# Prompt delta rule: the inverse turned instead of multiplied twice, and both lanes in the same step

## Chip, cores and metric

The kernel runs on one core of a Trainium2 chip. The metric is the time of one execution in device microseconds (us), lower is better. A core has five engines with a queue of instructions each: TensorE (PE, its weight loads are shown as PEld), VectorE (DVE), ScalarE (ACT), GpSimd (POOL) and SyncE (SP, which issues transfers). An engine takes its instructions in the order of the program and waits on semaphores.

## The reference, cut to what matters

The whole program is one inference step of a two-layer decoder. The change lies in layer 0, in the gated delta rule for the prompt: 512 tokens, 6 heads of 128, from a state of zeros.

```python
gamma = jnp.exp(jnp.where(incl, G[..., :, None] - G[..., None, :], -jnp.inf))
kk = jnp.einsum('nbhik,nbhjk->nbhij', kc, kc)
a_mat = jnp.where(strict, kk * gamma * bc[..., :, None], 0.0) + jnp.eye(chunk, dtype=F32)
rhs = jnp.concatenate([vc * bc[..., None], kc * (bc * jnp.exp(G))[..., None]], axis=-1)
sol = lax.linalg.triangular_solve(a_mat, rhs, left_side=True, lower=True, unit_diagonal=True)
u, w = sol[..., :DV], sol[..., DV:]
...
def step(S, xs):
    q_i, qk_i, u_i, w_i, k_i, d_i = xs
    e = u_i - jnp.einsum('bhck,bhkv->bhcv', w_i, S)
    o = jnp.einsum('bhck,bhkv->bhcv', q_i, S) + jnp.einsum('bhij,bhjv->bhiv', qk_i, e)
    S = S * d_i[..., None, None] + jnp.einsum('bhck,bhcv->bhkv', k_i, e)
    return S, o
```

What is computed per chunk and head is thus the inverse of a unit lower triangular matrix, applied to keys and values, and then one step of the state.

## The kernel before

The prompt's 512 tokens are 4 chunks of 128 (`NC_P`). The six heads are two lanes (`g` 0 and 1) of three heads each; every instruction of a lane covers its three heads (128x384 on DVE and ACT), and each product on PE is three 128x128 products in f32, which the trace shows as six records. The whole stage is one block (lines 1048 to 1224); the next begins when all engines have left it.

The inverse X of a chunk is doubled up in six levels (`NL` = 6, blocks of 2 to 64 rows). X and its transpose XT start at the first 2x2 blocks (`init`, DVE, lines 1190 to 1194). A level is two steps: `off` (line 1063: AT times X into bank 1 of PSUM; DVE then copies what lies under a mask into a step matrix, line 1185, `copy_predicated`) and `inv` (line 1074: the new X into bank 2; line 1076: the new XT into bank 3; ACT copies both to SBUF, lines 1153 and 1154). The last level computes XT alone.

Each chunk's matrix is made by the steps `ga`, `gb`, `gc`, `at` (products of lines 1084, 1087, 1090 and the transposes of line 1094; `ga` has three DVE operations, lines 1199 to 1202, and two exponentials on ACT, lines 1145 and 1146). Its result is used by `w`, `read`, `err`, `out`, `upd` (lines 1099 to 1121; `err` is two products per head). These nine "side" steps share bank 0 of their lane. On ACT `upd` also stands for three squares with sums (line 1166), which wait for `out`'s DVE part.

The order is written out by hand: `lane()` lists slots, each with one step of a level and perhaps a side step of the chunk before or after. `both_lanes` walks the slots, lane 1 one slot behind lane 0. All four engines follow this one order, each taking its own part of a step, so a step that waits holds up what stands behind it on its engine. In a chunk the slots carry `off`+`w`, `inv`+`read`, `off`+`err`, `inv`, `off`+`out`, `inv`+`ga`, `off`+`upd`, `inv`+`gb`, `off`, `inv`+`gc`, `off`+`at`, `inv`+`init` (`w` to `upd` of the chunk before, `ga` to `init` of the chunk after). GpSimd makes the scaled keys and values beside this (line 1133).

Of the kernel before, what the change touches and what calls it, by code (L numbers as in the profile page):

```python
# [13 lines left out]
ACT = mybir.ActivationFunctionType  # L14
# [7 lines left out]
NC_P = SEQ // P  # L22
# [90 lines left out]
def wait_after(eng, sem, value):  # L113

    if value > 0:
        eng.wait_ge(sem, value)


def build(nc, I, O, debug=()):
    ctx = ExitStack()  # L120
    with ctx:
# [17 lines left out]
        V, S, TE, G = nc.vector, nc.scalar, nc.tensor, nc.gpsimd  # L139
# [8 lines left out]
        ident, ones = const("ident"), const("ones")  # L148
# [517 lines left out]
        gb = sb("decays", [P, 8, NCH, DN_H], where=L0)  # L666
# [3 lines left out]
        NL = len(LV)  # L670
        spare = [ring[k][:, 768 * n:768 * (n + 1)] for k in range(2) for n in range(8)]
        spare = [v.rearrange("p (h t) -> p h t", h=DN_H) for v in spare]
        step_of = spare[0:NL]
# [142 lines left out]
        A, GT, AT, X, XT, Y = (x_flat[:, n * 768:(n + 1) * 768].rearrange("p (h t) -> p h t", h=DN_H) for n in range(6))  # L816
# [85 lines left out]
        def delta_solve(tag, c, r, pe_tail, dve_tail, act_tail, sync_tail, pool_tail):  # L902
# [4 lines left out]
            with nc.Block() as block:  # L907
# [96 lines left out]
        GH = DN_H // 2  # L1004
        GT2, AT2, XT2 = (GT, spare[NL]), (AT, spare[NL + 1]), (XT, spare[NL + 2])
        w_rows, e_rows = spare[NL + 3], spare[NL + 4]
        d_fill, d_free, d_off, d_inv, d_Z, d_X0, d_XT0, d_X, d_XT, d_A, d_G, d_exp, d_K, d_V, d_D, d_t = (
            [sem(f"delta_{m}{g}") for g in range(2)] for m in (
                "filled", "freed", "off_blocks", "inverses", "steps", "first_inverse", "first_inverse_T", "inverse", "inverse_T",
                "matrix", "gates", "exp", "beta_keys", "beta_values", "decayed_keys", "dve"))  # L1010
        s_zero = sem("state_zero")

        def group(t, g, rows=P):
            return t[:rows, GH * g:GH * (g + 1), :]

        def bank(k, g):

            return pp[k][:, 512 * g:512 * g + GH * P].rearrange("p (h t) -> p h t", h=GH)

        def lane():  # L1020


            yield from ([("ga", 0)], [("gb", 0)], [("gc", 0)], [("at", 0), ("init", 0)])
            for c in range(NC_P):
                for lv in range(NL):
                    off, inv = [("off", c, lv)], [("inv", c, lv)]
                    if c >= 1:
                        off += {0: [("w", c - 1)], 1: [("err", c - 1)], 2: [("out", c - 1)], 3: [("upd", c - 1)]}.get(lv, [])
                        inv += {0: [("read", c - 1)]}.get(lv, [])
                    if c + 1 < NC_P:  # L1030
                        off += {5: [("at", c + 1)]}.get(lv, [])
                        inv += {2: [("ga", c + 1)], 3: [("gb", c + 1)], 4: [("gc", c + 1)], 5: [("init", c + 1)]}.get(lv, [])
                    yield off
                    yield inv
            yield from ([(k, NC_P - 1)] for k in ("w", "read", "err", "out", "upd"))

        LANE = list(lane())
# [2 lines left out]

        def both_lanes(do):

            for t in range(len(LANE) + 1):
                for g in range(2):
                    for kind, c, *lv in LANE[t - g] if 0 <= t - g < len(LANE) else ():
                        do(g, kind, c, *lv)

        with nc.Block() as block:
            @block.tensor
            def _(pe):  # L1050
                def step(g, kind, c, lv=0):
                    tk = slice(offset(c), offset(c) + P)
                    hs = [(i, GH * g + i) for i in range(GH)]
                    b0 = bank(0, g)
                    at, xt, gt = AT2[c % 2], XT2[c % 2], GT2[c % 2]
                    if kind == "off":
# [5 lines left out]
                        for i, h in hs:  # L1062
                            ins = TE.matmul(bank(1, g)[:, i, :], at[:, h, :], X[:, h, :], start=True, stop=True)
                        ins.then_inc(d_off[g], 1)
                        return
                    if kind == "inv":
                        pe.wait_ge(d_Z[g], NL * c + lv + 1)
                        if lv == 0:
                            pe.wait_ge(d_XT0[g], c + 1)
                        else:  # L1070
                            pe.wait_ge(d_XT[g], NL * c + lv)
                        if lv < NL - 1:
                            for i, h in hs:
                                TE.matmul(bank(2, g)[:, i, :], xt[:, h, :], step_of[lv][:, h, :], start=True, stop=True)
                        for i, h in hs:
                            ins = TE.matmul(bank(3, g)[:, i, :], step_of[lv][:, h, :], xt[:, h, :], start=True, stop=True)
                        ins.then_inc(d_inv[g], 1)
                        return
                    if kind == "init":
                        return  # L1080
                    wait_after(pe, d_free[g], NTH[kind, c] - 1)
                    if kind == "ga":
                        for i, h in hs:
                            ins = TE.matmul(b0[:, i, :], bc(g_[:, c, h], 1, P), const("upper"), start=True, stop=True)
                    elif kind == "gb":
                        for i, h in hs:
                            ins = TE.matmul(b0[:, i, :], qkT[:, DN_H + h, tk], qkT[:, DN_H + h, tk], start=True, stop=True)
# [3 lines left out]
                    elif kind == "at":  # L1091
                        pe.wait_ge(d_A[g], c + 1)
                        for i, h in hs:
                            ins = TE.transpose(b0[:, i, :], A[:, h, :], ident)
# [41 lines left out]
            @block.scalar  # L1136
            def _(act):
                act.wait_ge(s_gs, 1)
                squares_at = itertools.count()

                def step(g, kind, c, lv=0):
                    at, xt, gt = (group(t[c % 2], g) for t in (AT2, XT2, GT2))
                    if kind == "ga":
                        act.wait_ge(d_G[g], c + 1)
                        act.activation(group(A, g), group(A, g), ACT.Exp, scale=-1.0).then_inc(d_exp[g], 1)
                        act.activation(gt, gt, ACT.Exp).then_inc(d_exp[g], 1)
                    elif kind == "at":
                        act.wait_ge(d_fill[g], NTH[kind, c])
                        act.activation(at, bank(0, g), ACT.Copy).then_inc(d_free[g], 1)
                    elif kind == "inv":  # L1150
                        act.wait_ge(d_inv[g], NL * c + lv + 1)
                        if lv < NL - 1:
                            act.activation(group(X, g), bank(2, g), ACT.Copy).then_inc(d_X[g], 1)
                        act.activation(xt, bank(3, g), ACT.Copy).then_inc(d_XT[g], 1)
                    elif kind == "w":
                        act.wait_ge(d_fill[g], NTH[kind, c])
                        act.activation(group(w_rows, g), bank(0, g), ACT.Copy, scale=-1.0).then_inc(d_free[g], 1)
                    elif kind == "err":
                        act.wait_ge(d_fill[g], NTH[kind, c])
                        act.activation(group(e_rows, g), bank(0, g), ACT.Copy).then_inc(d_free[g], 1)  # L1160
                    elif kind == "upd":
                        act.wait_ge(d_free[g], NTH["out", c])
                        for i in range(GH):
                            h = GH * g + i
                            wait_after(act, s_sq, next(squares_at))
                            act.activation(o_junk[:], rows_o[:, c, h * P:(h + 1) * P], ACT.Square, accum_out=gs[:, c, h:h + 1]).then_inc(s_sq, 1)

                both_lanes(step)

            @block.vector  # L1170
# [1878 lines left out]
```

## Time and profile before

| | us |
|---|---|
| three runs, median (lowest, highest) | 1743.87 (1740.88, 1750.09) |
| span of the profiled execution, first to last instruction | 1739.1 |
| PE busy in the span | 1475.6 (85%) |
| DVE, ACT busy in the span | 617.6, 384.5 |
| first product of the delta rule's stage, start of the stage after it | 317.4, 476.0 |

The profiled execution's time outside its span isn't recorded apart: the fastest run shown lies 1.8 us over the span and the median 4.8. A busy share over the whole span averages stages with different limits, so it is read by stretch. PE's end times are modelled; the starts of weight loads (PEld) are the better clock for when the queue moves on.

### The profile page before, as it was taken

Reading aid. Unit: us, or ns where it says so; the run is one execution under the profiler, and the core shown is the slowest. Engines: PE = TensorE matmul, PEld = TensorE weight load, DVE = VectorE, ACT = ScalarE, POOL = GpSimd, SP = SyncE. Lnnn points to the kernel's source line nnn. Section 1 sums busy time; section 2 is a strip of 40 time slices with the busy share of each in tenths; the row PEclk is TensorE's granted clock in tenths of the full one; section 3 lists DMA queues with packets and bytes.
Section 4 is the critical chain, followed back from the end, with each engine's and each line's share of the span. In section 5 each row is a group of like instructions: output and inputs, shape, how many; then the busy total and the mean of one; then the engine's idle time right before and its main releaser. Section 6 shows DMA issues by size and latency. Waiting matters only on the chain. (4 is left out here: it accounts for less than half of the span.)

```text
span 1739.1 us, 23072 instructions
## 1 busy us (share of the span) xinstructions
PE 1475.6 (85%) x9105; PEld 1003.8 (58%) x9105; DVE 617.6 (36%) x1410; ACT 384.5 (22%) x996; POOL 226.5 (13%) x227
## 2 busy tenths in 40 slices
PE   6999869899988886998886799999977977998880
PEld 3788756799966445554442566666655454554440
DVE  3455412456356114132111643445523141231114
ACT  2244203344422110111011212223413010111111
POOL 0000011111141001222221100001100001222213
PEclk9999969899976997999897899999988987999995
DMA  9611270000054527899995510403432466999984
GB/s 315 181 73 73 72 154 0 1 1 2 9 194 147 218 78 274 329 384 384 396 400 205 190 62 5 177 1 122 182 142 102 168 239 229 378 393 401 397 314 175
DMA packets 106935, 328.99 MB, mean 189 GB/s; under 512 B 19189, under 2 KB 59997, under 8 KB 81951
## 3 DMA queue, kind: packets, MB, share of 16 engines
q1 hardware_dynamic: 90546, 275.43, 43.1%
q0 software_dynamic: 15040, 47.74, 7.7%
q10 hardware_dynamic: 1248, 4.46, 0.6%
q8 instruction: 65, 1.06, 0.3%
q14 instruction: 36, 0.29, 0.1%
HBM read 301.46 MB, written 41.84 MB: 197 GB/s over the span
## 5 line engine op out<-in xcount | busy, mean ns | idle before, releaser
L1948 PE MATMUL pp<-ring,uT 128*64 128x256 f32 x1728 | 231.0, 410 | 35.6 <-issue 25.3
L1948 PEld LDWEIGHTS pp<-ring,uT 128*64 128x64 f32 x1728 | 124.4, 141 | 132.7 <-issue 65.9
L559 PE MATMUL pp<-uT,ring 128*128 128x272 f32 x576 | 135.2, 393 | 0.9 <-PEq L359 0.9
L559 PEld LDWEIGHTS pp<-uT,ring 128*128 128x128 f32 x576 | 108.0, 190 | 22.2 <-issue 1.0
L1630 PE MATMUL pp<-ring,uT 128*128 128x512 f32 x256 | 113.5, 606 | 4.2 <-PEq L135 4.2
L1969 PE MATMUL pp<-ring,uT 128*64 128x512 f32 x432 | 103.2, 598 | 1.2 <-ACT uT L1999 1.2
L1993 ACT ACTIVATE uT<-pp 128x128 f32<-128x128 f32 x64 | 17.7, 277 | 380.0 <-PE pp L1948 380.0
L1987 DVE COPY uT<-pp 128x128 f32<-128x128 f32 x64 | 18.6, 291 | 233.0 <-PE pp L1958 233.0
L2124 POOL DMA_INDIRECT expert_rows<-uT,row_of_slot x64 | 64.7, 1011 | 246.0 <-ACT uT L1999 242.2
L1630 PEld LDWEIGHTS pp<-ring,uT 128*128 128x128 f32 x256 | 49.7, 195 | 66.8 <-issue 66.8
L1936 PE MATMUL pp<-consts 64*128 64x64 f32 x512 | 70.3, 281 | 18.3 <-DMA consts<-normed_rows,token_of_slot 18.3
L2119 POOL DMA_INDIRECT consts<-normed_rows,token_of_slot x64 | 61.1, 955 | 183.2 <-PE pp L1936 122.9
L1936 PEld LDWEIGHTS pp<-consts 64*128 64x128 f32 x512 | 61.3, 200 | 27.0 <-issue 20.5
L1976 DVE TENSOR_TENSOR uT<-pp,gains 128x512 f32<-128x512 f32 x64 | 44.2, 691 | 76.7 <-PE pp L1936 76.7
L769 PE MATMUL pp<-ring,uT 128*128 128x512 f32 (+1 forms) x128 | 47.5, 530 | 15.9 <-PEq L512 15.9
L1999 ACT ACTIVATE uT<-pp 128x512 f32<-128x512 f32 x64 | 38.2, 597 | 98.2 <-PE pp L1969 98.2
L1969 PEld LDWEIGHTS pp<-ring,uT 128*64 128x64 f32 x432 | 31.2, 138 | 42.8 <-issue 34.4
L1982 DVE TENSOR_TENSOR uT<-uT,pp 128x128 f32<-128x128 f32 x64 | 18.4, 287 | 105.3 <-ACT uT L1993 105.3
L1948 PE MATMUL pp<-scaled_rows,uT 128*64 128x256 f32 x320 | 42.8, 410 | 11.2 <-issue 11.2
L1655 DVE TENSOR_TENSOR x<-x,pp 128x512 f32<-128x512 f32 x16 | 11.0, 686 | 103.8 <-PE pp L1630 94.5
L769 PEld LDWEIGHTS pp<-ring,uT 128*128 128x128 f32 x128 | 25.9, 207 | 33.7 <-issue 31.5
L2127 POOL MEMSET consts<- 64x2048 f32 x2 | 3.6, 1797 | 313.3 <-POOLq L292 313.3
(603 smaller groups left out, 2483.7 us busy)
## 6 DMA issues: line engine op xcount, KB each, us to landing
ring<-in_w_exp_gate SPq DMA_DIRECT2D x54, 1024.0 KB, 21.3
ring<-in_w_exp_up SPq DMA_DIRECT2D x54, 1024.0 KB, 27.7
ring<-in_w_exp_down SPq DMA_DIRECT2D x54, 1024.0 KB, 27.7
ring<-in_w_in_a SPq DMA_DIRECT2D x4, 3072.0 KB, 11.4
scaled_rows<-in_w_exp_gate SPq DMA_DIRECT2D x10, 1024.0 KB, 25.4
scaled_rows<-in_w_exp_up SPq DMA_DIRECT2D x10, 1024.0 KB, 29.6
expert_rows<-zero_rows SPq DMA_DIRECT2D x4, 2048.0 KB
scaled_rows<-in_w_exp_down SPq DMA_DIRECT2D x10, 512.0 KB, 22.2
```

The lines of the kernel that those rows point to most:

```text
L559: TE.matmul(pp[n % 2][:, at], w[:, j, ct * P:(ct + 1) * P], uT[:, j, t], start=(j == 0), stop=(j == DJ - 1))
L769: ins = TE.matmul(z_bank(p), uT[:, j, offset(c):offset(c) + P], w[:, j, z_cols[half]], start=(j == 0), stop=(j == DJ - 1))
L1630: ins = TE.matmul(pp[n // 2][:, (n % 2) * 512:(n % 2) * 512 + 512], mergedT[:, j, offset(c):offset(c) + P], w[:, j, :], start=(j == 0), st ...
L1936: ins = TE.transpose(pp[3][:, j * SLOTS:(j + 1) * SLOTS], xv[:, j, :], ident[:SLOTS, :SLOTS])
L1948: ins = TE.matmul(pp[0][q * SLOTS:(q + 1) * SLOTS, b * 512:b * 512 + 2 * P], xT[b][:, j, :], w[:, :, j, q, :], start=(j == 0), stop=(j == ...
L1969: ins = TE.matmul(pp[2][q * SLOTS:(q + 1) * SLOTS, 0:512], hT[b][:, j, :], w[:, q * 512:(q + 1) * 512], start=(j == 0), stop=(j == 1))
L1976: V.tensor_tensor(xT[b][:], pp[3][:, 0:DJ * SLOTS].rearrange("p (j t) -> p j t", j=DJ), bc(gains[:, G_FFN + l, :], 2, SLOTS), ALU.mult).th ...
L1982: V.tensor_tensor(hh[b][:], sg[b][:], pp[0][:, b * 512 + P:b * 512 + 2 * P], ALU.mult).then_inc(s.h, 1)
L1987: V.tensor_copy(hT[b][:], pp[1][:, 0:2 * SLOTS].rearrange("p (j t) -> p j t", j=2)).then_inc(s.hT, 1)
L1999: act.activation(yr[b][:], pp[2][:, 0:512], ACT.Copy).then_inc(s.y, 1)
L2119: pool.indirect_dma_start(xg[:, e % ROWS_IN, :], None, xs, bass.IndirectOffsetOnAxis(tok_i[:, e:e + 1], 0), bounds_check=T - 1, oob_is_err ...
L2124: pool.indirect_dma_start(ys.rearrange("r (q d) -> (r q) d", q=2), bass.IndirectOffsetOnAxis(out_i[:, e:e + 1], 0), yr[e % ROWS_OUT][:], None,
```

## The change

The product of line 1074 goes. In its place stands a step `back`: when ACT has copied the new XT to SBUF, PE transposes it (three transposes into bank 2) and ACT copies the result to X. The next level's `off` waits for that copy. The side steps are laid on the slots anew, now three in a level (`off`, `inv`, `back`), and both lanes take the same slot.

```diff
@@ -1004,9 +1004,9 @@
         GH = DN_H // 2
         GT2, AT2, XT2 = (GT, spare[NL]), (AT, spare[NL + 1]), (XT, spare[NL + 2])
         w_rows, e_rows = spare[NL + 3], spare[NL + 4]
-        d_fill, d_free, d_off, d_inv, d_Z, d_X0, d_XT0, d_X, d_XT, d_A, d_G, d_exp, d_K, d_V, d_D, d_t = (
+        d_fill, d_free, d_off, d_inv, d_back, d_Z, d_X0, d_XT0, d_X, d_XT, d_A, d_G, d_exp, d_K, d_V, d_D, d_t = (
             [sem(f"delta_{m}{g}") for g in range(2)] for m in (
-                "filled", "freed", "off_blocks", "inverses", "steps", "first_inverse", "first_inverse_T", "inverse", "inverse_T",
+                "filled", "freed", "off_blocks", "inverses", "turned_back", "steps", "first_inverse", "first_inverse_T", "inverse", "inverse_T",
                 "matrix", "gates", "exp", "beta_keys", "beta_values", "decayed_keys", "dve"))
         s_zero = sem("state_zero")
 
@@ -1022,16 +1022,13 @@
 
             yield from ([("ga", 0)], [("gb", 0)], [("gc", 0)], [("at", 0), ("init", 0)])
             for c in range(NC_P):
+                before = {("inv", 0): [("w", c - 1)], ("back", 0): [("read", c - 1)], ("inv", 1): [("err", c - 1)], ("back", 1): [("out", c - 1)],
+                          ("inv", 2): [("upd", c - 1)]} if c >= 1 else {}
+                after = {("back", 2): [("ga", c + 1)], ("inv", 3): [("gb", c + 1)], ("back", 3): [("gc", c + 1)], ("back", 4): [("at", c + 1)],
+                         ("inv", 5): [("init", c + 1)]} if c + 1 < NC_P else {}
                 for lv in range(NL):
-                    off, inv = [("off", c, lv)], [("inv", c, lv)]
-                    if c >= 1:
-                        off += {0: [("w", c - 1)], 1: [("err", c - 1)], 2: [("out", c - 1)], 3: [("upd", c - 1)]}.get(lv, [])
-                        inv += {0: [("read", c - 1)]}.get(lv, [])
-                    if c + 1 < NC_P:
-                        off += {5: [("at", c + 1)]}.get(lv, [])
-                        inv += {2: [("ga", c + 1)], 3: [("gb", c + 1)], 4: [("gc", c + 1)], 5: [("init", c + 1)]}.get(lv, [])
-                    yield off
-                    yield inv
+                    for kind in ("off", "inv", "back")[0:3 if lv < NL - 1 else 2]:
+                        yield [(kind, c, lv)] + before.get((kind, lv), []) + after.get((kind, lv), [])
             yield from ([(k, NC_P - 1)] for k in ("w", "read", "err", "out", "upd"))
 
         LANE = list(lane())
@@ -1040,9 +1037,9 @@
 
         def both_lanes(do):
 
-            for t in range(len(LANE) + 1):
+            for slot in LANE:
                 for g in range(2):
-                    for kind, c, *lv in LANE[t - g] if 0 <= t - g < len(LANE) else ():
+                    for kind, c, *lv in slot:
                         do(g, kind, c, *lv)
 
         with nc.Block() as block:
@@ -1067,14 +1064,18 @@
                         pe.wait_ge(d_Z[g], NL * c + lv + 1)
                         if lv == 0:
                             pe.wait_ge(d_XT0[g], c + 1)
+                            wait_after(pe, d_XT[g], NL * c)
                         else:
                             pe.wait_ge(d_XT[g], NL * c + lv)
-                        if lv < NL - 1:
-                            for i, h in hs:
-                                TE.matmul(bank(2, g)[:, i, :], xt[:, h, :], step_of[lv][:, h, :], start=True, stop=True)
                         for i, h in hs:
                             ins = TE.matmul(bank(3, g)[:, i, :], step_of[lv][:, h, :], xt[:, h, :], start=True, stop=True)
                         ins.then_inc(d_inv[g], 1)
+                        return
+                    if kind == "back":
+                        pe.wait_ge(d_XT[g], NL * c + lv + 1)
+                        for i, h in hs:
+                            ins = TE.transpose(bank(2, g)[:, i, :], xt[:, h, :], ident)
+                        ins.then_inc(d_back[g], 1)
                         return
                     if kind == "init":
                         return
@@ -1149,9 +1150,10 @@
                         act.activation(at, bank(0, g), ACT.Copy).then_inc(d_free[g], 1)
                     elif kind == "inv":
                         act.wait_ge(d_inv[g], NL * c + lv + 1)
-                        if lv < NL - 1:
-                            act.activation(group(X, g), bank(2, g), ACT.Copy).then_inc(d_X[g], 1)
                         act.activation(xt, bank(3, g), ACT.Copy).then_inc(d_XT[g], 1)
+                    elif kind == "back":
+                        act.wait_ge(d_back[g], (NL - 1) * c + lv + 1)
+                        act.activation(group(X, g), bank(2, g), ACT.Copy).then_inc(d_X[g], 1)
                     elif kind == "w":
                         act.wait_ge(d_fill[g], NTH[kind, c])
                         act.activation(group(w_rows, g), bank(0, g), ACT.Copy, scale=-1.0).then_inc(d_free[g], 1)
```

The slots of a chunk are now, level by level: `off`; `inv`+`w`; `back`+`read` | `off`; `inv`+`err`; `back`+`out` | `off`; `inv`+`upd`; `back`+`ga` | `off`; `inv`+`gb`; `back`+`gc` | `off`; `inv`; `back`+`at` | `off`; `inv`+`init`. The number of products is otherwise the same, and so are the DVE, GpSimd and ACT instructions; the transfers are untouched.

## Rows read from the trace of the kernel before

**Rows 1.** The page: busy time of each engine over the whole span.

```profile
...
PE 1475.6 (85%) x9105; PEld 1003.8 (58%) x9105; DVE 617.6 (36%) x1410; ACT 384.5 (22%) x996; POOL 226.5 (13%) x227
```

**Rows 2.** Stretches A:B: length, busy by engine, TensorE clock share, DMA share, GB/s.

```profile
...
317.40:326.00 8.60, 6.56 (x27) 5.98 (x28) 5.48 (x10) 2.22 (x3) 5.46 (x6) 0.50 0.00 1
...
334.00:360.30 26.30, 24.72 (x214) 23.95 (x212) 12.97 (x25) 10.64 (x25) 0.00 (x0) 1.00 0.01 1
360.30:465.60 105.30, 104.98 (x924) 103.96 (x924) 57.43 (x113) 47.86 (x128) 14.64 (x18) 1.00 0.01 1
...
472.00:476.00 4.00, 2.19 (x16) 1.69 (x14) 2.28 (x7) 2.55 (x13) 0.00 (x0) 1.00 0.00 0
```

**Rows 3.** Groups by line, 328 to 466 us: busy, mean ns, idle before.

```profile
...
L1185 DVE COPY_PREDICATED ring<-consts,pp 128x384 f32<-128x384 uint32 x48 | 27.7, 585 | 26.5 <-PE pp L1063 25.5
...
L1074 PE MATMUL pp<-ring,x 128*128 128x128 f32 x120 | 17.1, 278 | 1.0 <-DVE ring L1185 1.0
```

**Rows 4.** Timeline at 462.7 us: start, length, engine, line, operation, [idle before <-releaser].

```profile
...
462.76 0.49 ACT L1153 ACTIVATE x<-pp 128x384 f32<-128x384 f32 x1 [2.08 <-PE pp L1076]
...
463.31 0.74 PEld L1063 LDWEIGHTS pp<-x,ring 128*128 128x128 f32 x6
...
464.09 0.74 PEld L1099 LDWEIGHTS pp<-ring,uT 128*128 128x128 f32 x6
...
464.28 0.59 DVE L1185 COPY_PREDICATED ring<-consts,pp 128x384 f32<-128x384 uint32 x1 [2.37 <-PE pp L1063]
464.92 0.74 PEld L1076 LDWEIGHTS pp<-ring 128*128 128x128 f32 x6
...
465.89 0.49 ACT L1154 ACTIVATE ring<-pp 128x384 f32<-128x384 f32 x1 [0.34 <-PE pp L1076]
```

**Rows 5.** Timeline at 392 us: three transposes, then a product of three heads.

```profile
...
392.05 0.36 PEld L1094 LDWEIGHTS pp<-consts,x 128*128 128x128 f32 x3
...
392.38 0.75 PEld L1074 LDWEIGHTS pp<-ring 128*128 128x128 f32 x6
...
392.69 0.49 ACT L1149 ACTIVATE x<-pp 128x384 f32<-128x384 f32 x1 [1.47 <-PE pp L1094]
393.05 0.75 PEld L1076 LDWEIGHTS pp<-ring 128*128 128x128 f32 x6
```

**Rows 6.** Timeline, 341 to 344.5 us: the `ga` step of one lane.

```profile
...
341.18 0.75 PEld L1084 LDWEIGHTS pp<-consts,decays 128*128 128x128 f32 x6
...
342.16 0.56 DVE L1199 TENSOR_TENSOR x<-pp,decays 128x384 f32<-128x384 f32 x1 [2.86 <-PE pp L1084]
...
343.82 1.05 DVE L1185 COPY_PREDICATED ring<-consts,pp 128x384 f32<-128x384 uint32 x2
343.94 0.52 ACT L1145 ACTIVATE x<-x 128x384 f32<-128x384 f32 x1 [1.58 <-DVE ring L1202]
...
344.45 0.74 PEld L1074 LDWEIGHTS pp<-ring,x 128*128 128x128 f32 x6 [1.18 <-DVE ring L1185]
```

**Rows 7.** Timeline at 349.9 us: a product behind ScalarE's exponentials.

```profile
...
349.91 0.74 PEld L1063 LDWEIGHTS pp<-x 128*128 128x128 f32 x6 [0.69 <-ACT x L1153]
```

**Rows 8.** Timeline, 328 to 330.2 us: one lane's `init`, the first `off`.

```profile
...
328.02 0.55 DVE L1190 TENSOR_TENSOR x<-x,consts 128x384 f32<-128x384 f32 x1
...
329.29 0.74 PEld L1063 LDWEIGHTS pp<-x 128*128 128x128 f32 x6 [0.97 <-issue]
...
330.15 0.55 DVE L1210 TENSOR_TENSOR x<-x,pp 128x384 f32<-128x384 f32 x1
```

**Rows 9.** Timeline at 455.9 us: squares on ScalarE.

```profile
...
455.87 0.31 ACT L1166 ACTIVATE o_junk<-qkv_rows 128x128 f32<-128x128 f32 x1
...
456.31 0.31 ACT L1166 ACTIVATE o_junk<-qkv_rows 128x128 f32<-128x128 f32 x1
```

**Rows 10.** Timeline at 476 us: the next stage begins.

```profile
...
476.02 0.45 PEld L917 LDWEIGHTS pp<-consts,decays 32*32 32x32 f32 x12 [1.38 <-issue]
```

**Rows 11.** Timeline at 317.4 us: a product of three heads at the low clock.

```profile
...
317.38 1.36 PEld L1084 LDWEIGHTS pp<-consts,decays 128*128 128x128 f32 x6 [3.31 <-issue]
```

## The prediction

> **What bounds the kernel now.** I read the page first: PE is busy for 85% of the span and no other engine for more than 36% [rows 1]. That is an average over many stages, so next I read the delta rule's stage by stretches. The reader is to see that from 334 us PE is busy for 24.72 of 26.30 us and then for 104.98 of 105.30, at full clock and with no transfers to speak of, while DVE and ACT work about half of the time [rows 2]. So this stage is bound by PE, and by nothing else. Nothing is loaded during it, so what the stage gains or loses the whole kernel does: the next stage starts at 476.02, when every engine is through [rows 10]. The groups by line say the same from the other side: DVE's masked copies wait 26.5 us for PE, and PE waits about 1 us for them [rows 3].
>
> **What goes.** A product of three heads holds PE's queue for 0.67 us (weight loads at 392.38 and 393.05), three transposes for 0.33 (392.05 to 392.38) [rows 5]. There are 4 chunks x 5 levels x 2 lanes = 40 products of line 1074, and 40 `back` steps in their place: 40 x 0.34 = 13.4 us less PE work. If PE stayed the bound, this would be the gain. Every other product, DVE and ACT operation stays, so the remaining question is what the new order makes PE wait for.
>
> **The chain of a level.** Prices of its steps: a product's result is taken up 0.98 us after its first weight load (463.31 to 464.28 on DVE, 464.92 to 465.89 on ACT), the masked copy takes 0.58, an ACT copy 0.49, and PE starts 0.06 after either (463.25 to 463.31, 464.87 to 464.92) [rows 3, 4]. Three transposes are taken up after 0.64 (392.05 to 392.69) [rows 5]. No row shows a transpose in this very place; the same operation between products bounds it from both sides, no less than 0.33 of queue and no more than a whole product's 0.98 to the reader. I take 0.64; by the other end it would be 0.34 more on each bare level.
> Before, `off` to the next `off` is off 0.98, masked copy 0.58 + 0.06, inverse 0.98, ACT 0.49 + 0.06 = 3.15, and both lanes give PE 6 x 0.67 = 4.02: PE is the longer. Now `back` is inside the chain: 3.15 + 0.64 + 0.49 + 0.06 = 4.34 us, against 3.34 of PE work for both lanes. So a level without side steps takes 4.34 instead of 4.02. The product taken away doesn't shorten it; it becomes a wait of 1.0.
>
> **Where PE waits in the new order** (in us of wait, all worked with the prices above; PE's work itself is already counted):
> - Bare levels, with no side step beside `inv` and `back`: levels 0 and 1 of chunk 0, levels 3 and 4 of chunk 3. 4 x 1.0 = 4.0. Level 2 of chunk 0 has only `ga`: 0.45.
> - Levels 0 and 1 of chunks 1 to 3 have side steps in both slots, which cover everything but the way from `off` to `inv`: 1.62 against the 1.34 of two `off`s. 6 x 0.28 = 1.7.
> - Level 2 of chunks 1 to 3 has `upd`. Its squares on ACT (three at 0.44 each, 1.3 per lane [rows 9]) now stand for both lanes between the copies of XT and the copy of X, so the next `off` waits for ACT: 0.75 in chunks 1 and 2 (of it 0.28 as above), 2.1 in chunk 3, where no `ga` fills PE. 3.6.
> - Level 3 of chunks 0 to 2: `ga` of both lanes comes right before the masked copies of level 3 on DVE. One `ga` holds DVE for 1.66 us (342.16 to 343.82), and before the change one alone already let PE wait 1.18 [rows 6]. Now: `back` of lane 0 at 0, its `ga` at 0.33, taken up at 1.31, two of them until 4.63, masked copy and start of `inv` at 5.27. PE's own work is done at 3.34 to 3.81. Waits 1.9, 1.4, 1.4. In parallel lane 1's copy of X stands on ACT behind lane 0's exponentials, as it did before for a wait of 0.69 [rows 7]; it ends before DVE does and adds nothing. 4.8.
> - Level 4 (`at` in its last slot): 0.28 before `inv`, 0.18 before `back`. 3 x 0.46 = 1.4. Level 5: ACT's four copies in a row make lane 1 late, 3 x 0.42 + 0.28 = 1.5.
> - From chunk to chunk. `init` is four DVE operations, 2.13 us (328.02 to 330.15) [rows 8]. Before, the lag of the lanes kept masked copies between the two `init`s. Now DVE has both, 4.26 us, before the first masked copy of the new chunk. With level 5's last product off PE's queue at E, the first `init` starts at E - 0.84, the masked copy at E + 3.42, `inv` at E + 4.06. PE has two `off`s, 1.34. Wait 2.7, of which 0.28 is counted above for level 0. 3 x 2.46 = 7.4.
>
> Sum 4.0 + 0.45 + 1.7 + 3.6 + 4.8 + 1.4 + 1.5 + 7.4 = 24.8 us. Before, from the first `off` at 329.29 to lane 0's last `w` at 464.09 are 134.8 us [rows 4, 8], and the work in it is 4 x (5 x 4.02 + 2.68) + 3 x 12.7 for the side steps, less 0.3 for the lag, 129.0: 5.8 us of waits, gone with the old order.
> At the edges: both `init`s in front of chunk 0 put the walk's start 1.6 later; at the end no lane lags, which saves one slot with what it waits for, 1.6. Nothing together.
> **Balance: -13.4 + 24.8 - 5.8 = +5.6 us.** The profiled span of 1739.1 becomes 1744.7; on the runs' scale, median 1743.87, 1749.5 us. That is 0.3%; about 0.5%, 8.7 us, is what a measurement of this kernel can tell from no change, so my forecast is "no change, on the slow side".
> The new waits `back` for ACT stand at the head of PE's queue: behind them stands the other lane's `back` and the side steps, on which DVE and GpSimd wait; these have slack (GpSimd's six operations of a chunk take 5.5 us of 35 or more, by the stretch from 317.4 us [rows 2]). SyncE issues nothing in the stage.
>
> **Rivals.**
> 1. PE stays the bound. The waits of DVE and ACT fall inside PE's work, as nearly all did in the old order (DVE sat idle half of the stage [rows 2]). Then -13.4 us: 1730.5. Against it: the two pairs on DVE, `ga` + `ga` and `init` + `init`, are in the program's order, and the chain of 4.34 leaves no room in a bare level.
> 2. The clock falls: slower for certain. At a chunk's end PE issues 1.34 us of work in 4.06, and a pause of 3.31 us ahead of the stage was followed by half clock, 0.50 in the records (1.2 GHz), for the next 8.6 us [rows 2, 11], with a product at 1.36 us instead of 0.67. For it to decide, such a chunk end must do what that pause did. For: a third busy is far below the old stage from 334 us on [rows 2]. Against: the longest single pause in the new order is 1.5, and in 472 to 476 PE was busy 2.19 of 4 us and kept 1.00 [rows 2]. If all three chunk ends do it, each costs some 9 us at half clock, in which about 6.5 us of full-clock work take twice as long less the 2 us of waits they swallow, 4.5: +13.5 on top, 1763.
> 3. Transposes leave the clock to fall in bare levels. Worked from rows: with half clock a product holds the queue for 1.36 [rows 11], and a bare level of both lanes is at least 6.7 us of PE work instead of 4.34, +2.3 for some 5 levels: +11.5, 1761. Against it: transposes are 0.67 of a bare level's 3.34, so matmuls still fill 2.7 of 4.34, more than the 2.19 of 4 that kept the clock at 1.00 [rows 2].
> The Trainium skill, "TensorE: Matmul & The Clock Gate", section "Part 4: PE-mode transpose", says that a transpose doesn't bring the full clock as a product does; by that rule rival 3 could come true. No row before isolates it.
> 4. One of the two DVE pairs costs nothing, because an operation slides past: -5 or -7 from the forecast, 1743.5, no change.
>
> **How the numbers follow.** The forecast has 0.64, with a range of its own of 1744 to 1755 (each of the 24 level waits may be off by 0.1 to 0.2): 0.54 of it within 0.5%, 0.10 slower. Rival 1 has 0.12 (0.11 faster), rival 2 has 0.14 (0.13 slower; one or two falls lie between 1754 and 1759), rival 3 0.04 (slower), rival 4 0.06 (same). Faster 0.11, same 0.62, slower 0.27. The range 1739 to 1761 leaves out rival 1 and the worst of rival 2, some 0.17.
>
> **What would show it.** In the changed kernel's timeline: groups of transposes 40 times (120 records of `back`), line 1074's 240 gone; a period of lane 0's `w` from chunk to chunk near 38.2 us (the old order's work alone is 22.8 + 12.7 = 35.5); bare levels 4.3 apart; before each new chunk PE waiting for DVE twice to three times, 2.7 us in all, behind eight DVE operations of `init` in a row; at level 3 a wait of 1.4 to 1.9 for the masked copy behind six operations of `ga`; PE busy near 85% of the stage, where it was 98%. It is wrong if the period of a chunk is at or under 36, if PE shows no waits for DVE at `init`, or if the granted clock in the stage leaves 1.00.

## The result and the profile after

The changed kernel takes 1753.36 us (median of 8 runs, 1749.47 to 1756.04), the kernel before 1742.66 (8 runs) on the same chip: 1.0055 times as long, 95% interval 1.004 to 1.0069. Run once more beside other kernels it was 1.0042 times as long (1.0023 to 1.0061). The forecast was 1749.5 with a range of 1739 to 1761, "no change, on the slow side". The time is inside that range and near the upper end of 1744 to 1755, the range given to the sum itself. As a difference it is 10.7 us against 5.6 forecast, and over the 8.7 us that the forecast took for the least that can be told from no change.

The page of the changed kernel, span and first row, to be held against [rows 1]:

```profile
span 1752.7 us, 22832 instructions
...
PE 1481.8 (85%) x8985; PEld 1002.4 (57%) x8985; DVE 618.1 (35%) x1410; ACT 386.3 (22%) x996; POOL 226.8 (13%) x227
```

PE's share of the span is the same 85%: at this distance nothing is to be seen. The stretches of the delta rule's stage, from the first `off` to lane 0's first `w`, then from `w` to `w`, then to the end (length, busy by engine, TensorE clock share, DMA share, GB/s), answer to [rows 2]:

```profile
...
330.10:366.70 36.60, 31.44 (x234) 28.96 (x235) 21.37 (x40) 12.85 (x28) 0.00 (x0) 0.95 0.00 1
366.70:408.40 41.70, 38.04 (x290) 36.37 (x290) 21.45 (x42) 16.89 (x44) 4.83 (x6) 0.91 0.00 1
408.40:447.50 39.10, 35.45 (x290) 33.79 (x290) 21.43 (x42) 16.89 (x44) 4.84 (x6) 0.97 0.00 1
447.50:487.30 39.80, 37.37 (x303) 34.41 (x301) 13.77 (x30) 18.71 (x54) 4.84 (x6) 1.00 0.00 1
```

The stage lasts from 318.66 to 487.34 us, 168.7 instead of 158.6 [rows 10, 11]. Two things are new. PE is no longer busy all of the time: its weight loads fill 36.37 of 41.70 us and 33.79 of 39.10. And the clock column, 1.00 everywhere in the old stage from 334 us [rows 2], says 0.95, 0.91, 0.97.

The timeline at the first new chunk, lane 0's `init` on DVE from 360.91, lane 1's from 363.02 (line 1060 is `off`, 1071 `inv`, 1100 `w`):

```profile
...
360.91 0.54 DVE L1192 TENSOR_TENSOR x<-x,consts 128x384 f32<-128x384 f32 x1
...
362.15 0.74 PEld L1060 LDWEIGHTS pp<-x,ring 128*128 128x128 f32 x6 [0.34 <-issue]
...
363.02 0.55 DVE L1192 TENSOR_TENSOR x<-x,consts 128x384 f32<-128x384 f32 x1
...
364.28 0.74 PEld L1060 LDWEIGHTS pp<-x,ring 128*128 128x128 f32 x6 [1.38 <-issue]
...
365.14 1.04 DVE L1187 COPY_PREDICATED ring<-consts,pp 128x384 f32<-128x384 uint32 x2
365.77 1.02 PEld L1071 LDWEIGHTS pp<-ring 128*128 128x128 f32 x6 [0.75 <-DVE ring L1187]
...
366.67 1.40 PEld L1100 LDWEIGHTS pp<-x,uT 128*128 128x128 f32 x6
```

This is the place that the forecast walked through: PE idle 0.34, 1.38 and 0.75 us, 2.5 together against 2.7 forecast, because eight `init` operations stand on DVE in a row. The last row shows what the sum had not priced: `w`'s weight loads last 1.40 us for six, where six last 0.75 at full clock. The granted clock went to its lower level (1.2 GHz) at 366.17 us, after the three pauses, when the work was back, and stayed there for 3.4 us. At the next chunk, behind the same three pauses, it fell again (407.13); at the last one, behind the same pauses once more, it did not.

Level 3 of the same chunk (line 1201 is the first operation of `ga`, 1187 the masked copy):

```profile
...
385.29 0.56 DVE L1201 TENSOR_TENSOR x<-pp,decays 128x384 f32<-128x384 f32 x1
...
385.98 0.75 PEld L1060 LDWEIGHTS pp<-x,ring 128*128 128x128 f32 x6
...
387.11 0.55 DVE L1201 TENSOR_TENSOR x<-pp,decays 128x384 f32<-128x384 f32 x1
...
388.59 0.74 PEld L1060 LDWEIGHTS pp<-x,ring 128*128 128x128 f32 x6 [1.86 <-ACT x L1156]
...
388.76 0.59 DVE L1187 COPY_PREDICATED ring<-consts,pp 128x384 f32<-128x384 uint32 x1
...
389.41 0.79 PEld L1071 LDWEIGHTS pp<-ring 128*128 128x128 f32 x6
```

Lane 1's `off` waits 1.86 us for its X, which stands on ACT behind lane 0's exponentials; the masked copy waits for both `ga`s (385.29, 387.11) until 388.76; `inv` starts at 389.41. Next come two bare levels, `off` to `off`:

```profile
...
337.09 1.49 PEld L1060 LDWEIGHTS pp<-x 128*128 128x128 f32 x12
...
341.36 1.49 PEld L1060 LDWEIGHTS pp<-x 128*128 128x128 f32 x12
```

4.27 us apart; 4.34 was forecast for the chain. PE's waits by what ended them, from the first `inv` to the end:

```profile
...
PEld pp L1060 <- ACT x L1156: 6.6, 4, 1.9
...
PEld pp L1071 <- DVE ring L1187: 5.2, 18, 0.7
PEld pp L1060 <- issue: 5.2, 6, 1.4
```

("issue" is the two `off`s of a new chunk, whose first blocks come from DVE's `init`.) The first and the third line belong to the lockstep (both lanes in the same slot). Of the second, the three waits of 0.75 us at a new chunk do; the rest is the way from `off` to `inv`, and with the lanes apart again such waits come to 7.6 us in 17 places (run lag_turn below).

### The profile page after: what moved, and what is told of

It reads as the page before. It is cut to its first block and busy times, and to the rows that moved or that the text cites. A ratio compares the mean times of both kernels' runs of the same rounds, so it can differ in the third digit from the quotient of the medians.

```text
span 1752.7 us, 22832 instructions
## 1 busy us (share of the span) xinstructions
PE 1481.8 (85%) x8985; PEld 1002.4 (57%) x8985; DVE 618.1 (35%) x1410; ACT 386.3 (22%) x996; POOL 226.8 (13%) x227
## 5 line engine op out<-in xcount | busy, mean ns | idle before, releaser
L2001 ACT ACTIVATE uT<-pp 128x512 f32<-128x512 f32 x64 | 38.2, 598 | 97.4 <-PE pp L1971 97.4
```

Of the source, the lines that this page charges most:

```text
L2001: act.activation(yr[b][:], pp[2][:, 0:512], ACT.Copy).then_inc(s.y, 1)
```

## The experiments

Stage lengths below are from the first weight load of `ga` to the first of the next stage in the profiled execution; "low" is the time that the clock stood at half between the first `off` and the end of the stage (twice the missing share of a stretch times its length: 41.7 us at 0.91 are 7.5); "chunk" is the distance between lane 0's `w` of chunks 0 and 1, then 1 and 2. Ratios are against the kernel before, run in turn on the same chip. "Lag" has lane 1 one slot behind lane 0, "lockstep" has both in the same slot; "product" makes X by a second product, "turn" transposes XT. Every kernel with the turn also has the new places of the side steps, and no run separates these two. Stage, low and chunk are of one execution each; the ratio is of all.

| kernel | lanes | X from | ratio (95%) | stage | low | chunk |
|---|---|---|---|---|---|---|
| before | lag | product | 1 | 158.6 | 0 | 36.1, 36.1 |
| changed | lockstep | turn | 1.0055 (1.004 to 1.0069) | 168.7 | 13.6 | 41.7, 39.1 |
| changed again | lockstep | turn | 1.0042 (1.0023 to 1.0061) | 165.4 | 6.8 | 39.4, 38.1 |
| fill | lockstep | turn | 1.0034 (1.0014 to 1.0054) | 163.1 | 0 | 38.1, 38.1 |
| lock_product | lockstep | product | 1.0016 (1.0005 to 1.0028) | 164.8 | 3.4 | 38.2, 38.2 |
| xt_pool | lockstep | turn | 1.006 (1.0039 to 1.0081) | 163.0 | 3.4 | 37.8, 37.8 |
| lock_exp | lockstep | turn | 1.0052 (1.0034 to 1.007) | 169.8 | 17.1 | 40.0, 41.0 |
| lock_split | lockstep | turn | 1.0023 (1.0011 to 1.0034) | 162.1 | 3.4 | 37.5, 37.5 |
| lag_turn | lag | turn | 1.0004 (0.9993 to 1.0014) | 161.1 | 0 | 36.6, 36.6 |
| before_exp | lag | product | 1.0004 (0.999 to 1.0019) | 158.3 | 0 | 36.0, 36.0 |
| lag_exp | lag | turn | 0.9975 (0.9961 to 0.9988) | 155.1 | 0 | 35.0, 35.0 |
| lag_exp_mix | lag | both | 0.9974 (0.9958 to 0.9989) | 153.8 | 0 | 35.0, 35.0 |

The stage is the sharper measure. What lies before and after it is the same code in all twelve traces and still varies: the start of the stage from 317.2 to 320.4, what follows it from 1259 to 1266 us (1275 once). Of the 13.6 us between the two first spans 10.0 are in the stage.

**fill.** Products that nobody reads, in PE's waits:

```diff
+                def fill(k, n):
+                    for _ in range(n):
+                        TE.matmul(pp[k][:, GH * P:512], ident, ident, start=True, stop=True)
...
+                        if g == 1 and lv == 0:
+                            fill(2, 6)
+                        if g == 1 and lv == 3 and c + 1 < NC_P:
+                            fill(3, 8)
+                        if g == 0 and lv == 0:
+                            fill(2, 3)
```

> The changed kernel with products of the identity with itself, which nobody reads, put into PE's waits: 6 before lane 1's off and 3 before lane 0's inv at level 0, 8 before lane 1's off at level 3, each 0.22 us at full clock and so just inside the waits. Theory (the pauses let the clock fall for 3.4 us at a time, each fall costing about 1.6 us beyond the pause): granted clock 1.00 from level 0 of chunk 0 on; the waits stay as long as they were; stage 4 to 6 us shorter, near 163, total near 1748. Rival (the clock's falls cost nothing, PE had to wait there anyway): same as the changed kernel within 1.5 us, or slower by what the fillers add.

Its stretches, first `off` to `w`, then `w` to `w`:

```profile
...
330.60:366.20 35.60, 35.10 (x285) 32.71 (x286) 21.30 (x40) 13.05 (x28) 0.00 (x0) 1.00 0.00 1
366.20:404.30 38.10, 37.89 (x324) 36.55 (x323) 21.45 (x42) 16.88 (x44) 4.84 (x6) 1.00 0.01 1
404.30:442.40 38.10, 37.89 (x324) 36.56 (x323) 21.45 (x42) 16.88 (x44) 4.84 (x6) 1.00 0.01 2
```

The clock stays at 1.00 and the stage is 163.1 us, 5.6 less than in the first run of the changed kernel, though PE has more to do. The distance between chunks is 38.10, twice; the forecast's period was 38.2. So the forecast's walk was right for a full clock, and the rest is the clock: 5.6 us for 13.6 us of half clock, 6.7 for the 17.1 of lock_exp, 2.3 for the 6.8 of the second run, 0.34 to 0.41 us lost for each. The second run of the changed kernel says the same without any added product: its second distance, at full clock throughout, is 38.1 too.

This holds for the one execution that was traced. Over all runs fill is 1.0034 times as long (1.0014 to 1.0054), and its interval overlaps both of the changed kernel's: seven of its twelve times lie between 1744.0 and 1746.5, five between 1753.1 and 1760.0, and the trace is of one of the seven (1745.5). That the added products keep the clock up in every execution is not shown.

**lock_product.** The kernel before, with `both_lanes` of the changed one:

```diff
-            for t in range(len(LANE) + 1):
+            for slot in LANE:
                 for g in range(2):
-                    for kind, c, *lv in LANE[t - g] if 0 <= t - g < len(LANE) else ():
+                    for kind, c, *lv in slot:
```

> The kernel before (two products a level, old slots) with both lanes in the same slot. Theory: PE has 4.02 us of work a level and side products also between off and inv, which cover most of the same two DVE pairs; about 1.4 us of wait at each new chunk, none at ga, 0.28 in some eight levels: 6 to 7 us of waits against 5.8 before. Same as before within 2 us (1741 to 1746), clock 1.00 in the stage. Rival (lockstep by itself is what costs): 5 us or more slower than before, with falls of the clock.

The theory's number was wrong here. By the stage the rival was right: 164.8 us, 6.2 more than before (some 1.2 of it one fall of the clock behind the first `init` pair). By the runs the kernel lies between the two, 1.0016 times as long, 1 to 5 us. A new chunk, lane 0's and lane 1's `off` (line 1063), each with its `w` (1099), then `inv` (1074):

```profile
...
403.55 0.74 PEld L1063 LDWEIGHTS pp<-x 128*128 128x128 f32 x6 [0.30 <-issue]
...
404.21 0.75 PEld L1099 LDWEIGHTS pp<-ring,uT 128*128 128x128 f32 x6
...
405.68 0.74 PEld L1063 LDWEIGHTS pp<-x 128*128 128x128 f32 x6 [0.71 <-issue]
...
406.34 0.75 PEld L1099 LDWEIGHTS pp<-ring,uT 128*128 128x128 f32 x6
...
407.80 0.74 PEld L1074 LDWEIGHTS pp<-ring,x 128*128 128x128 f32 x6 [0.71 <-DVE ring L1185]
```

I had counted both `w`s as cover for the `init` pair. Lane 1's `w` stands in PE's queue behind lane 1's `off`, which waits for `init`, so it covers nothing until 406.34. Lockstep costs 2.1 us a chunk in the old kernel as well.

**lag_turn.** The opposite edit on the changed kernel: its `back` and its slots, with lane 1 a slot behind.

> The changed kernel with lane 1 one slot behind lane 0 again; the turning and the new slots stay. Theory (lanes in lockstep put two init and two ga side by side on DVE, and these waits let the clock fall): the waits of PE for DVE at each new chunk (2.5 us) and at level 3 (1.4 to 1.9 us) go, the granted clock stays at 1.00 from the first level on, and only bare levels wait (about 4.6 us a level for 3.34 of work). Waits in the stage near 12 us instead of 25: the stage falls from 168.7 us to about 150 to 153, under the 158.6 of the kernel before; total near 1735 to 1738. Rival (the turn itself costs, since PE's queue stands behind ACT's copy of XT at every level, whatever the lanes do): the stage stays at 165 us or more, total 1750 or more.

The direction came, the size didn't. The clock holds 1.00 and of the 2.5 us at each new chunk 0.5 are left, but the stage is 161.1, not 150 to 153. By the runs it equals the kernel before (1.0004, 0.9993 to 1.0014, clear of both intervals of the changed kernel), and its stage is 2.4 longer. PE's remaining waits and the place of the longest (line 1077 is `back`):

```profile
...
PEld pp L1077 <- ACT x L1153: 6.1, 4, 2.0
...
PEld pp L1077 <- ACT ring L1153: 2.7, 2, 1.4
```

```profile
...
381.24 0.75 PEld L1071 LDWEIGHTS pp<-ring 128*128 128x128 f32 x6
...
382.73 0.56 DVE L1204 SCALAR_TENSOR_TENSOR x<-x,consts 128x384 f32<-128x384 f32 x1
...
383.32 0.52 ACT L1146 ACTIVATE x<-x 128x384 f32<-128x384 f32 x1 [2.19 <-DVE x L1204]
...
384.17 0.47 ACT L1153 ACTIVATE ring<-pp 128x384 f32<-128x384 f32 x1
...
384.69 0.31 PEld L1077 LDWEIGHTS pp<-consts,ring 128*128 128x128 f32 x3 [1.36 <-ACT ring L1153]
```

Lane 1's `inv` was issued at 381.24, so its result was there at 382.2; ACT copies XT (line 1153) only at 384.17, after the exponentials of lane 0's `ga`, which waited for DVE until 383.3. With two products this copy is nobody's hurry: X was copied first and `off` waited for that alone. With the turn XT is on the chain, and 8.8 us of waits hang on it.

**lag_exp.** The exponentials get a step of their own, one slot later on ACT:

```diff
-            yield from ([("ga", 0)], [("gb", 0)], [("gc", 0)], [("at", 0), ("init", 0)])
+            yield from ([("ga", 0), ("exp", 0)], [("gb", 0)], [("gc", 0)], [("at", 0), ("init", 0)])
...
-                after = {("back", 2): [("ga", c + 1)],
+                after = {("back", 2): [("ga", c + 1)], ("off", 3): [("exp", c + 1)],
...
-                    if kind == "ga":
+                    if kind == "exp":
                         act.wait_ge(d_G[g], c + 1)
```

> The changed kernel with lane 1 one slot behind again and, alone beside that, the exponentials of ga taken up by ACT one slot later (with off of level 3). Theory (with the lag, what is left is lane 1's copy of XT behind the exponentials, 8.8 us of PE's waits in six places of the run with the lag alone): these go, the stage falls from 161.1 to 153 to 155 us, 4 us or more under the kernel before (158.6); total 1737 to 1740 where before has 1744. Rival (the wait only moves, since the copy of X or the masked copy is late next): stage 159 us or more.

```profile
...
360.90:395.90 35.00, 34.20 (x291) 32.51 (x290) 20.96 (x43) 17.28 (x45) 5.11 (x6) 1.00 0.00 1
395.90:430.90 35.00, 34.19 (x291) 32.51 (x290) 20.96 (x43) 17.28 (x45) 5.12 (x6) 1.00 0.01 2
```

155.1 us, 6.0 under lag_turn and 3.5 under the kernel before; 0.9975 of its time. A chunk takes 35.0 instead of 36.1, with 32.5 us of weight loads where the old kernel has 35.7 in 36.1. The rival, 159 or more, is out.

**before_exp.** The same move in the kernel before.

> The kernel before with the exponentials of ga one slot later on ACT. Theory: PE is the bound there, its waits behind the exponentials are 0.7 us in one place: stage 157.5 to 158.6, total the same as before within 1.5 us. Rival (the exponentials cost as much here as with the turn): 3 us or more faster.

158.3 us, 1.0004 of the time (0.999 to 1.0019). With the lag, the exponentials matter with the turn and not without it.

**lock_exp.** The same move in the changed kernel, lanes in lockstep.

> The changed kernel (lanes in lockstep) with only the exponentials of ga one slot later on ACT. Theory (in lockstep the pair of ga on DVE is the later of two causes at level 3, so the exponentials add nothing of their own): lane 1's off of level 3 starts 1.9 us earlier, lane 0's inv not at all; the distance from chunk to chunk at full clock stays at 38.1 us within 0.3, stage 163 to 169 by the falls of the clock. Rival (the exponentials are the cause here as they were with the lag, 6 us over the stage): 36.5 us or less from chunk to chunk, stage under 162.

```profile
...
386.14 1.42 PEld L1060 LDWEIGHTS pp<-x,ring 128*128 128x128 f32 x12
...
388.46 0.56 DVE L1204 SCALAR_TENSOR_TENSOR x<-x,consts 128x384 f32<-128x384 f32 x1
388.93 1.05 DVE L1187 COPY_PREDICATED ring<-consts,pp 128x384 f32<-128x384 uint32 x2
...
389.56 0.74 PEld L1071 LDWEIGHTS pp<-ring 128*128 128x128 f32 x6 [2.00 <-DVE ring L1187]
```

Lane 1's `off` follows lane 0's at once (twelve loads from 386.14), and `inv` starts at 389.56, 3.42 after lane 0's `off`, as in the changed kernel (389.41 - 385.98 = 3.43). The forecast's claim that lane 1's copy of X "ends before DVE does and adds nothing" holds in lockstep. The expected distance of 38.1 at full clock can't be read here, since this execution had 17.1 us of half clock and no distance without some of it; its stage, 169.8, is 0.8 over the expected 163 to 169.

**lock_split.** Beside that, `ga`'s second and third DVE operations behind the masked copy:

```diff
-                        dve.wait_ge(d_free[g], NTH[kind, c])
+                    elif kind == "exp":
+                        dve.wait_ge(d_free[g], NTH["ga", c])
                         d(V.scalar_tensor_tensor(A_, Y_, 0.0, masks["lower_big"], ALU.max, ALU.add))
```

> As the run before, and of ga's three DVE operations the second and third too are taken up one slot later, behind level 3's masked copy of their lane. Theory (DVE's pair of ga is what level 3 waits for): lane 0's inv of level 3 starts 1.2 to 1.7 us earlier, lane 1's waits 0.3 instead; chunk to chunk 36.9 to 37.3 us at full clock, stage 3 us shorter than in the run before at equal falls of the clock, 159.5 to 165. Rival (the wait moves on to gb and gc, which need the exponentials): chunk to chunk 38 or more.

37.5 from chunk to chunk, 0.6 less than 38.1: the right direction, half of the size. DVE's pair was the wait before `inv` (line 1071): lane 0's now starts 1.6 us behind its `off` (384.24 to 385.86) instead of 3.4. But level 3 still takes 7.5 us to the next `off` instead of 8.1, for 6.0 of work, and the trace shows what came in between:

```profile
...
388.83 0.51 ACT L1147 ACTIVATE x<-x 128x384 f32<-128x384 f32 x1
...
389.25 0.85 ACT L1153 ACTIVATE ring<-pp 128x384 f32<-128x384 f32 x2
...
389.77 0.31 PEld L1077 LDWEIGHTS pp<-consts,ring 128*128 128x128 f32 x3 [0.96 <-ACT ring L1153]
```

`inv` is earlier, but ACT copies XT only behind both lanes' exponentials, and `back` waits 0.96 us for that copy. It is the wait of lag_turn again: neither the theory (DVE's pair alone) nor the rival (`gb` and `gc` need the exponentials) had it.

**xt_pool.** `init`'s second half on GpSimd:

```diff
-                        dve.wait_ge(d_free[g], NTH["at", c])
-                        d(V.tensor_tensor(xt, at, masks["level1T"], ALU.mult))
-                        V.tensor_tensor(xt, xt, masks["ident"], ALU.add).then_inc(d_XT0[g], 1)
...
+                        pool.wait_ge(d_free[g], NTH["at", c])
+                        first[g](G.tensor_tensor(xt, at, bc(const("level1T"), 1, GH), ALU.mult))
+                        G.tensor_tensor(xt, xt, bc(ident, 1, GH), ALU.add).then_inc(d_XT0[g], 1)
```

> The changed kernel with the second half of init (first blocks of XT, two of the four DVE operations) on GpSimd. Theory (DVE's pair of inits is the wait at a new chunk): the pair takes 2.1 us less on DVE, so inv of a new chunk starts some 2 us earlier, 6 us over three chunks; with shorter pauses the clock falls at fewer chunk ends, another 0 to 3 us. Stage 160 to 163 us, total near 1745. Rival (the wait at a new chunk is for ACT's copies or for the matrix of the next chunk, not for DVE): within 2 us of the changed kernel.

The stage, 163.0, is in the expected range, but the chunk distance says why that isn't the theory's doing: 37.8, only 0.3 less than at full clock with both halves on DVE. And by the runs it is no faster than the changed kernel (median 1755.18 where about 1745 was expected), which is the rival's number, though not for the rival's reason. GpSimd and DVE beside each other:

```profile
...
359.10 1.00 POOL L1136 TENSOR_TENSOR ring<-ring,consts 128x384 f32<-128x384 f32 x1
...
359.89 0.62 DVE L1205 TENSOR_TENSOR x<-x,consts 128x384 f32<-128x384 f32 x1
...
360.06 1.32 POOL L1135 TENSOR_TENSOR ring<-ring,consts 128x384 f32<-128x384 f32 x1
...
360.55 1.24 DVE L1206 TENSOR_TENSOR x<-x,consts 128x384 f32<-128x384 f32 x1
...
361.46 1.20 POOL L1136 TENSOR_TENSOR ring<-ring,consts 128x384 f32<-128x384 f32 x1
...
361.72 1.35 DVE L1205 TENSOR_TENSOR x<-x,consts 128x384 f32<-128x384 f32 x1
...
363.11 0.56 DVE L1206 TENSOR_TENSOR x<-x,consts 128x384 f32<-128x384 f32 x1
```

A DVE operation of `init` takes 0.55 when GpSimd is idle [rows 8]. Of the four that stay on DVE, the two that began early in one of GpSimd's took 1.24 and 1.35 us, and the last, after GpSimd was done, 0.56. Each of the three that began inside a GpSimd operation ended 0.41 us after it (360.10 to 360.51, 361.38 to 361.79, 362.66 to 363.07). So of the 2.2 us taken off DVE 1.5 came back. The Trainium skill, "SBUF — State Buffer", section "Who interferes with whom", says that a DVE instruction with two SBUF inputs and a GpSimd operation that reads SBUF exclude each other; the trace agrees, 1.24 against 0.55.

**lag_exp_mix.** lag_exp, with the second product kept where a level is bare:

```diff
+        BARE = ((0, 0), (0, 1), (NC_P - 1, 3), (NC_P - 1, 4))
...
+                        if (c, lv) in BARE:
+                            for i, h in hs:
+                                TE.matmul(bank(2, g)[:, i, :], xt[:, h, :], step_of[lv][:, h, :], start=True, stop=True)
```

> As the run with lag and later exponentials, but in the four bare levels (0 and 1 of chunk 0, 3 and 4 of chunk 3) X is the second product again instead of the turned XT. Theory (a bare level is bound by the chain, 4.3 to 4.6 us with the turn, and by PE, 4.0 to 4.3, with the product): 0.3 us a level less, the stage 1 to 1.5 us shorter than with the turn everywhere. Rival (turning is never worse): the same or longer by up to 2.7 us, the products' added work.

```profile
...
329.70:360.80 31.10, 29.97 (x242) 27.97 (x243) 19.95 (x38) 13.01 (x29) 0.00 (x0) 1.00 0.00 1
360.80:395.80 35.00, 34.20 (x291) 32.51 (x290) 20.97 (x43) 17.28 (x45) 5.11 (x6) 1.00 0.00 1
```

153.8 us, 1.3 under lag_exp: where nothing else is there to do, PE's extra product is shorter than the turn's longer chain. Median 1737.84, against 1743.35 for the kernel before and 1739.97 for lag_exp; by the runs the two can't be told apart, by the stage of the one traced execution each they can. It has the shortest stage of all: 4.8 us less in the stage than before and 14.9 less than in the changed kernel.

**The changed kernel again.**

> The changed kernel once more, beside the others of this job. 8 to 11 us slower than before (ratio near 1.006). In its trace: stage between 163 us (if the clock doesn't fall after the first level) and 169; 1.4 to 1.7 us for every 3.4 us at the lower clock between the first level and the end.

165.4 us, with 6.8 us at half clock instead of 13.6. The same program meets the falls in different numbers from execution to execution; between the two traces that is 3.3 us of stage, a part of its spread of 1742.81 to 1755.82; the rest isn't traced. In the medians it is 8.2 us over the kernel before, by the ratio 4 to 11, a little under the 8 to 11 expected.

## Why the prediction was right, and where it was not

- **Work removed, 13.4 us.** Right: 120 transposes stand where 240 records of line 1074 were, and three take 0.33 us. (40 x 0.34 as written is 13.6; 13.4 comes from 0.67 and 0.33 before rounding.)
- **The bare chain, 4.34 us.** Right: 4.27.
- **From chunk to chunk, 2.7 us.** Right: 2.5, in three pieces and for the reason given (xt_pool alone doesn't prove DVE, since GpSimd spoils it; the rows of the timeline and lag_turn, where 0.5 is left with the pair apart, do).
- **Levels 2 and 3.** In chunk 0 level 3 costs the 1.9 forecast. In chunks 1 and 2, at full clock, it takes 8.1 us for 6.0 of work, a wait of 2.1 and not 1.4. In fill, `off` of level 3 and of level 4:

```profile
...
384.15 0.75 PEld L1068 LDWEIGHTS pp<-x,ring 128*128 128x128 f32 x6
...
392.24 0.86 PEld L1068 LDWEIGHTS pp<-x,ring 128*128 128x128 f32 x7
```

- In return level 2 was priced too high in these chunks, 0.75 against 0.3 (6.3 us for 6.0 of work), so the two errors largely cancel; that the distance came out at 38.1 is in this part luck. That DVE's pair decides in lockstep is right (lock_exp, lock_split), though most of the wait stands before lane 1's `off` (1.86) and not before `inv`. In lag_turn, where the pair is apart, the exponentials decide.
- **The sum.** Chunk to chunk 38.2 forecast, 38.1 measured at full clock. The stage of fill is 4.5 us longer than before, forecast 5.6: the walk was 1.1 too long, 0.6 of it at the squares of chunk 3 (1.5 instead of 2.1).
- **The clock.** This is what the prediction had wrong. The sum puts it at nothing, and the prediction's own last sign of being wrong, "if the granted clock in the stage leaves 1.00", came. Rival 2 had the mechanism, chance 0.14, but with another size: some 9 us of half clock and 4.5 us lost at a chunk end, 13.5 for all three, and 1754 to 1759 for one or two. The trace of the changed kernel has four falls of 3.4 us after the first `off`, 13.6 us together, at 1.4 us lost each: one behind the `init` pair in front of chunk 0 (332.0), two at chunk ends (366.2, 407.1) and one at level 3 (390.1); rival 2 had looked at the chunk ends alone. The two of the second run cost 1.2 each. I had argued that no single pause exceeds 1.5 us; the longest is 1.86, at level 3, and at the chunk ends falls came behind three shorter ones close together. In the first execution the clock is worth 5.6 us, more than the 4.5 that all the rest comes to; together they are the 10.0 by which the stages differ. The forecast came out because its range was wide enough for a term that it didn't contain, and because a fall cost a third of rival 2's price. That is luck; the waits, the period and the direction are not.
- **Rival 1** (PE stays the bound) is refuted by every lockstep run. **Rival 3** (transposes leave the clock to fall) too: lag_turn, lag_exp and lag_exp_mix have the transposes and keep 1.00 from the first `off` to the end, bare levels included (in lag_exp_mix alone these have the product), and in the changed kernel the bare levels of chunk 3 lie in a stretch of 1.00. The rule of the Trainium skill, "TensorE: Matmul & The Clock Gate", section "Part 4: PE-mode transpose", decides nothing here: no run has transposes alone, and among products the clock stayed at 1.00 in these three. **Rival 4** is out: both pairs cost.
- **Not foreseen:** that lockstep, not the turn, is the greater part of the loss. From lag_turn to the changed kernel only the lag goes, and the runs go from 1.0004 to 1.0055 and 1.0042. In stage times at full clock or near it: lag and product 158.6, lag and turn 161.1, lockstep and product 164.8 (3.4 us low), lockstep and turn 163.1. The turn with its new slots, the exponentials where they were, loses 2.4 instead of gaining 13.4 less the bare levels (nothing that the runs can tell); with them moved it gains 3.5, and 0.9975 by the runs.

What stays open: why the clock falls behind the same pauses at one chunk and not at the next, and in one execution and not in another; what share of the loss the new places of the side steps have; and the 8 to 10 us by which the two groups of fill's times differ, since no trace is of the longer one. (What follows the stage differs by 6 us in eleven of the traces; in lock_exp it is 9 longer than the longest of these.)

## What to carry to other kernels

Where one engine is the bound, taking work off it is worth only what its queue can use: first lay out the new chain of one round and the longest run of operations on each other engine between two of its steps. Two lanes in the same step put the same long operation twice in a row on the helper engine; a lag of one slot hides it, here 6 us of 159. And when a value that was a by-product comes onto the chain, look at what stands before its copy: with the lag the same edit (exponentials one slot later) was worth 6.0 us of the stage after the change and 0.4 before it, and in lockstep it moved nothing, because another wait ended later.

## What the runs showed of the hardware

- Short pauses of PE (0.34, 1.38 and 0.75 us within 4 us, with work between them) were followed by half clock at two of three chunk ends of one execution, and at one of three in the second. A fall lasted 3.4 us and cost 1.2 to 1.4. In the one traced execution with products without a use in these pauses the clock stayed at 1.00 and the stage was 5.6 us shorter; over all runs no gain is shown.
- DVE operations with two SBUF operands took 1.24 to 1.35 us instead of 0.55 while GpSimd worked on SBUF tensors of the same size, and ended 0.41 us after GpSimd's.
